# S5 output sums laid between the first steps of the triangular inverses, GLU blocks behind the products with the inverse

## The reference

```python
# gated DeltaNet: 4 heads of 128 channels, chunks of 64 tokens
lower = jnp.where(strict, einsum('bhnid,bhnjd->bhnij', k_beta, k) * decay, 0.0)
sol = triangular_solve(lower + eye, [v * beta, k_beta * exp(gc)])      # u, w
attn = einsum('bhnid,bhnjd->bhnij', q, k) * decay
# for each chunk:
v_new = u_i - w_i @ state
o = qd_i @ state + attn_i @ v_new
state = state * sd_i + kd_i.T @ v_new
# S5: 32 groups of 16 channels, each with 64 complex states
y = Re(C x) + D u ;  y = gelu(y) ;  y = y * sigmoid(y @ glu_w + glu_b)
# the two halves are concatenated and projected
return concatenate([rms_norm(o) * silu(z), y]) @ w_out
```

## Time and profile before

| what | value |
|---|---|
| median of 3 runs | 1383.79 us (1382.90 to 1386.55) |
| the profiled execution | 1378.0 us |
| its span, first to last instruction | 1376.4 us |
| PE busy | 1318.1 us, 96% |
| VectorE busy | 710.2 us, 52% |
| the changed stretch, 202 to 306 us | 104 us; PE busy 95.8, VectorE 70.8 |
| mean granted clock of PE | 0.98 |

### The profile page before, as it was taken

How to read it: one execution, slowest core, us unless ns; L and a number is a source line. 1 busy time by engine, 2 the same in 40 slices (tenths; PEclk the granted TensorE clock), 3 DMA queues, 4 the chain that set the end, 5 groups by cost and what they waited for, 6 DMA issues and landing times.

```text
span 1376.4 us, 18845 instructions
## 1 busy us (share of the span) xinstructions
PE 1318.1 (96%) x7511; PEld 1098.4 (80%) x7511; DVE 710.2 (52%) x796; ACT 504.4 (37%) x590; POOL 137.5 (10%) x225
## 2 busy tenths in 40 slices
PE   5899999899899999999999999999999999999997
PEld 3588888898778888888787888887778888888886
DVE  3789867476756633446636243345563333333353
ACT  6344642353422221222323276455432232222232
POOL 6007986000000000000000000000000000000000
PEclk9999999999899999999998999999999999999999
DMA  9484553306267642357422320211233323433122
GB/s 316 141 153 154 178 137 82 94 19 227 62 218 240 222 137 84 108 151 233 149 78 90 117 67 31 85 47 54 73 97 106 92 69 92 115 104 108 58 80 77
DMA packets 201547, 163.25 MB, mean 119 GB/s; under 512 B 25422, under 2 KB 191531, under 8 KB 199435
## 3 DMA queue, kind: packets, MB, share of 16 engines
q1 hardware_dynamic: 198256, 136.24, 34.3%
q0 software_dynamic: 2720, 25.99, 5.2%
q10 hardware_dynamic: 506, 0.12, 0.1%
HBM read 157.21 MB, written 4.19 MB: 117 GB/s over the span
## 4 chain that ended last, share of the span: by engine, by line
PE 88%; DVE 4%; ACT 2%; issue 2%; SPq 2%; DMA 1%; DVEq 0%; ACTq 0%
PE banks L487 26%; PE banks L489 25%; PE banks L488 25%; PE banks L783 2%; PE banks L1135 1%; PE banks L1108 1%; DMA ada_first<-in_ada_w_dram 1%; PE banks L493 1%; SPq L374 1%; PE banks L1126 1%; PE banks L1125 1%; SPq L348 1%; PE banks L831 1%; PE banks L773 1%; PE banks L705 0%
## 5 line engine op out<-in xcount | busy, mean ns | idle before, releaser
L487 PE MATMUL banks<-hn_hi,whi 128*128 128x512 f32 x992 | 393.4, 397 | 11.0 <-DVE hn_lo L1778 7.4
L489 PE MATMUL banks<-hn_hi,wlo 128*128 128x512 f32 x992 | 389.6, 393 | 0.0
L488 PE MATMUL banks<-hn_lo,whi 128*128 128x512 f32 x992 | 389.5, 393 | 0.0
L1756 DVE TENSOR_TENSOR wlo<-raw,whi 128x2048 fp32r<-128x2048 f32 (+3 forms) x110 | 234.0, 2129 | 124.3 <-ACT whi L1319 60.0
L1319 ACT ACTIVATE whi<-raw 128x2048 fp32r<-128x2048 f32 (+1 forms) x66 | 123.1, 1865 | 315.0 <-PE banks L489 314.8
L487 PEld LDWEIGHTS banks<-hn_hi,whi 128*128 128x128 f32 x992 | 188.7, 190 | 51.3 <-issue 11.7
L489 PEld LDWEIGHTS banks<-hn_hi,wlo 128*128 128x128 f32 x992 | 188.2, 190 | 39.8
L488 PEld LDWEIGHTS banks<-hn_lo,whi 128*128 128x128 f32 x992 | 188.9, 190 | 38.3
L487 PE MATMUL banks<-ff_hi,whi 128*128 128x512 f32 x416 | 165.7, 398 | 2.4 <-DVE ada_acc L2174 1.6
L489 PE MATMUL banks<-ff_hi,wlo 128*128 128x512 f32 x416 | 162.2, 390 | 0.0
L488 PE MATMUL banks<-ff_lo,whi 128*128 128x512 f32 x416 | 162.1, 390 | 0.0
(11 more groups left out here) (450 smaller groups left out, 1638.5 us busy)
## 6 DMA issues: line engine op xcount, KB each, us to landing
raw<-in_ffn_w_in_dram SPq DMA_DIRECT2D x88, 512.0 KB, 4.6
ada_in<-in_ada_w_dram POOLq DMA_DIRECT2D x16, 1536.0 KB, 6.3
ada_in<-in_ada_w_dram SPq DMA_DIRECT2D x24, 512.0 KB, 4.3
raw<-in_ffn_w_out_dram SPq DMA_DIRECT2D x32, 384.0 KB, 3.8
raw<-in_sb_w_in_dram SPq DMA_DIRECT2D x24, 512.0 KB, 4.1
raw<-in_hy_w_in_dram SPq DMA_DIRECT2D x20, 512.0 KB, 6.0
raw<-in_ffn_w_out_dram SPq DMA_DIRECT2D x32, 320.0 KB, 3.3
ada_first<-in_ada_w_dram SPq DMA_DIRECT2D x8, 1024.0 KB, 15.1
```

What stands on the lines that cost most here:

```text
L487: pe.matmul(o, lh, rh, start=first, stop=False)
L488: pe.matmul(o, lh, rl, start=False, stop=False)
L489: return pe.matmul(o, ll, rh, start=False, stop=last)
L1756: TTO(wlo[s][:, 0:width], raw[s][:, 0:width], whi[s][:, 0:width].bitcast(F32), SUB)\
```

## The change

1. The table `GDN_STAGES` loses `y`, and `at` moves behind `d2`, `d2t`. The S5 sums now go to banks 0 to 3.
2. The S5 sums become a function `s5_outputs(r)`, and its eight steps are laid behind `d2`/`d2t` (0, 1), `at` (2), `x1` (3, 4), `d4` (5, 6) and `x2` (7).
3. The tiles `Da`, `DaT`, `Db`, `DbT`, `X`, `XT`, `Z` move to the unused upper halves of the weight slots, so slots 12 and 13 are loaded and split later.
4. `DaT` is made by VectorE between the drains of `lt` and `l`.
5. Six tiles of the modulation and the scaling of the queries move between VectorE's drains of the inverse; the eight `mod_column` products stand together behind `z2`.
6. `u` and `w` are drained by VectorE, ahead of `ys_lo`. The GLU blocks stand behind `w` and ahead of the chunk loop.
7. On VectorE the splits of the gated S5 half (`mixed_lo`) and of slots 12 and 13 stand inside the chunk loop.

```diff
-GDN_STAGES = [("gr",), ("kt", "vt"), ("lt",), ("at",), ("y",), ("l",),
-              ("d2", "d2t"), ("x1",), ("d4", "d4t"), ("x2",), ("d8t",), ("x3",), ("xt",),
+GDN_STAGES = [("gr",), ("kt", "vt"), ("lt",), ("l",),
+              ("d2", "d2t"), ("at",), ("x1",), ("d4", "d4t"), ("x2",), ("d8t",), ("x3",), ("xt",),
...
-        Da, DaT, Db, DbT, X = (diagonal(n, o) for n, o in (("Da", 120), ("DaT", 104), ("Db", 136),
-                                                           ("DbT", 144), ("X", 128)))
+        Da, DaT, Db, DbT, X = (diagonal(n, o) for n, o in (("Da", 20), ("DaT", 28), ("Db", 36),
+                                                           ("DbT", 44), ("X", 52)))
...
             for t in range(8):
                 ada0_tile(4, t)
+            sp.wait_ge(s5_copied, 8)
             for i in range(SC):
-                if i == 0:
-                    for q in range(4):
-                        wait_drained(sp, "y", q)
...
+            sp.wait_ge(gdn_done, GDN_AT[("d8t", NH - 1)] + 1)
             for s in range(2):
                 load_slot(12 + s, s, cols(hy_w_out[0], 256 * s)(s))
...
@@ tensor @@
-                if lv == 1:
-                    pe.wait_ge(ys_done, 1)
-                    pe.wait_ge(mod_done, 3)
-                    four_blocks(10, B_GLU, ys_hi, ys_lo, k_tiles=4)
...
+            pe.wait_ge(ys_done, 1)
+            pe.wait_ge(mod_done, 3)
+            four_blocks(10, B_GLU, ys_hi, ys_lo, k_tiles=4)
 
             for c_ in range(TT):
                 for hd in range(NH):
...
-                        pe.wait_ge(block_free, B_OUT0)
+                        pe.wait_ge(block_free, B_GLU + hd + 1)
...
@@ scalar @@
-            for hd in range(NH):
-                drain_scaled("u", hd, vn, k_gain)
-                drain("w", hd, wT)
...
@@ vector @@
+            lt_drained(0)
+            lt_drained(1)
+            lower_turned(0)
+            lt_drained(2)
+            lower_turned(1)
+            lt_drained(3)
+            lower_turned(2)
+            l_drained(0)
+            lower_turned(3)
...
             onto("x2", X, ADD)
+            ada0_tile(4, 2)
             onto("x3", X, ADD)
+            ada0_tile(4, 3)
             masked(0)
+            ada0_tile(4, 4)
             onto("xc0", X, SUB)
+            ada0_tile(4, 5)
             onto("xtc0", XT, SUB)
+            masked(1)
+            ada0_tile(4, 6)
+            onto("xc1", X, SUB)
+            ada0_tile(4, 7)
...
+            lo(10, 0, 1024)
+            for hd in range(NH):
+                src, free = product("u", hd)
+                TTO(vn[:, hd, :, :], src, bc(k_gain[:, hd, :], P), MUL).then_inc(free, 1)
+                src, free = product("w", hd)
+                dve.tensor_copy(wT[:, hd, :, :], src).then_inc(free, 1)
+            lo(11, 1, 1024)
...
             for c_ in range(TT):
...
+                if c_ == 1:
+                    for r in range(4):
+                        mixed_lo(r)
+                if c_ == 2:
+                    lo(12, 0)
+                    lo(13, 1)
```

More of the change, by code:

```diff
@@ L836, in _ @@
                               start=False, stop=False)
-                for o, rows, i, g in lanes(r):
+                for o, rows, i in lanes:
                     last = pe.matmul(o[:, 0:wide * NC].rearrange("p (a c) -> p a c", c=NC)[:, :, 1:NC],
@@ L841, in _ @@
                     if r == 7:
-                        last.then_inc(gdn_done, 1)
+                        last.then_inc(s5_sum, 1)
             for hd in range(NH):
@@ L855, in _ @@
                 mul_pair("x1", hd, DbT, X)
-                if hd == 0:
-                    pe.wait_ge(block_free, B_Z + 4)
-                    pe.wait_ge(ada_used, 24)
-                for k in range(2 * hd, 2 * hd + 2):
-                    last = mod_column(3, 4, k, ada0_acc[0])
-            last.then_inc(mod_sum, 1)
+            s5_outputs(3)
+            s5_outputs(4)
             for hd in range(NH):
@@ L898, in _ @@
                     o[64:P, 0:64], LT[0:64, hd, c_, 64:P], X[0:64, hd, c_, :], start=True, stop=True))
+            pe.wait_ge(s5_copied, 8)
+            pe.wait_ge(ada_used, 24)
+            for k in range(KT):
+                last = mod_column(3, 4, k, ada0_acc[0])
+            last.then_inc(mod_sum, 1)
             for hd in range(NH):
@@ L1488, in _ @@
                 drain_pair("d8t", hd, DbT)
+            for n in range(4):
+                act.wait_ge(s5_sum, 5 + n)
+                act.activation(u_pair[:, 8 * (n // 2):8 * (n // 2) + 8, n % 2, :],
+                               bank[n].rearrange("p (g c) -> p g c", c=NC), ACT.Copy).then_inc(s5_copied, 1)
             for hd in range(NH):
                 drain_pair("xt", hd, XT)
+            hi(10, 0, 1024)
+            hi(11, 1, 1024)
+            act.preload_act_table(ACT.Gelu_apprx_tanh)
             act.wait_ge(y_in, 64)
@@ L1503, in _ @@
                 act.activation(perm(ys_hi[:, r, :]), y_s5[:, r, :, :], ACT.Copy).then_inc(glu_hi, 1)
+            act.wait_ge(gdn_done, GDN_AT[("xtc2", NH - 1)] + 1)
             hi(12, 0)
             hi(13, 1)
-            for hd in range(NH):
-                drain_scaled("u", hd, vn, k_gain)
-                drain("w", hd, wT)
             for hd in range(NH):
@@ L2009, in _, with pair, each, lt_drained @@
                 dve.tensor_copy(k_tok[:, hd, :, :], src).then_inc(free, 1)
-            for t in range(2, 4):
-                ada0_tile(4, t)
-            for hd in range(NH):
+            def pair(name, hd):
+                q, b, _ = gp(name, hd)
+                dve.wait_ge(gdn_done, q + 1)
+                return bank[b][:, 0:256].rearrange("p (c i) -> p c i", c=TT), drained[q % 4]
+            def each(m_):
+                return m_[:, 0:64].unsqueeze(1).to_broadcast([P, TT, 64])
+            def lt_drained(hd):
                 src, free = product("lt", hd)
@@ L2087, in _, with mixed_lo @@
                 TS(XTF[0:64, hd, :, 64:P], src[0:64, :, 64:P], -1.0, None, MUL).then_inc(free, 1)
-            lo(12, 0)
-            lo(13, 1)
-            for r in range(4):
+            mod_parts(2, 4, 1)
+            lo(10, 0, 1024)
+            for hd in range(NH):
+                src, free = product("u", hd)
[3 more added lines that the diff above has]
+            lo(11, 1, 1024)
+            dve.wait_ge(ys_hi_done, 1)
+            TTO(ys_lo[:, :, :], y_s5[:, :, :, :].rearrange("p k j c -> p k (j c)"),
+                ys_hi[:, :, :].bitcast(F32), SUB).then_inc(ys_done, 1)
+            dve.wait_ge(scan_done, 1)
+            dve.memset(sq_sum[:, :], 0.0).then_inc(sq_added, 8)
+            for r in range(4):
+                dve.wait_ge(block_free, B_GLU + r + 1)
+                TTO(y_s5[:, r, :, :], y_s5[:, r, :, :], tmp[r % 2][:, :].rearrange("p (j c) -> p j c", j=SC),
+                    MUL).then_inc(glu_mul, 1)
+            dve.wait_ge(glu_mul, 4)
+            def mixed_lo(r):
                 dve.wait_ge(glu_hi, r + 1)
@@ L2445, in _ @@
                 select(dec[:, hd, :, :], [[0, TT], [1, P]], 0, -1).then_inc(dec_done, 1)
-            for hd in range(NH):
-                wait_drained(pool, "lt", hd)
-                wait_drained(pool, "at", hd)
-                for n, rows in enumerate((slice(0, 64), slice(64, P))):
-                    pool.tensor_tensor(DaT[rows, hd, :, :], LT[rows, hd, :, rows],
-                                       strict_upper[rows, :].unsqueeze(1).to_broadcast([64, TT, 64]), MUL)\
-                        .then_inc(dat_done, 1)
-                    pool.wait_ge(dat_done, 2 * hd + n + 1)
             pool.wait_ge(gates, 1)
@@ L2463, in _ @@
             pool.wait_ge(rk_done, NH)
-            pool.wait_ge(gdn_done, GDN_AT[("d8t", NH - 1)] + 1)
+            pool.wait_ge(s5_sum, 8)
             pool.memset(XTF[64:P, :, :, 0:64], 0.0).then_inc(xt_zero, 1)
```

110 lines of the change are left out of this document (49 added, 61 removed).

## The result

The changed kernel takes 1401.9 us (median of 4 runs, 1397.3 to 1403.7), the kernel before on the same chip 1383.35: ratio 1.0134, 95% interval 1.0103 to 1.0166, 18.5 us slower. Forecast were 1398.5 and a range of 1389 to 1405.

A forecast was written before the change was run, and what follows sets the result against it. PE, busy 96% of the span, was taken to bound the kernel. Terms of 0.6 + 2.9 + 8.2 + 3 = 14.7 us, with the runs' offset carried over, gave 1398.5 us, 1.1% slower; 8-in-10 range 1389 to 1405 us.

The forecast's parts named there:

- Third part: Chunk loop: PE waits 3.4 and 4.2 us for drains queued behind VectorE's splits, last drains 0.6; +8.2 us.
- Second part: u, w and GLU: PE waits 4.3 us for ys_lo and 1.0 for the last sigmoid; +2.9 us in sum.
- First part: From lt to the end of the inverse: 4.3 us removed, 6.4 added, 1.5 of issue gaps saved; +0.6 us.
- rival D: Ahead of d2: S5 steps hide no wait; DaT at twice 0.43 us gives 1402 us; 11% shared with Rival B.
- The issue gaps: Long run of 64x64 products, line 783: 3.5 us of gaps now, 2 taken as left, saving 1.5 us.
- The clock: PE's lower clock after three new idle stretches (GLU, chunk loop): 0 to 7 us, 3 taken.
- Rival B: Ahead of GLU: stored S5 results return late, excess over 2 us margin counts; 1407.5 us; 11% shared with rival D.
- A: Whole stretch: waits as worked out, but clock stays up and issue gaps vanish; +8.3 us, 1392 us; 12%.
- C: Chunk loop and GLU wait: not slower, VectorE's late passes are short; +2.2 us, 1386 us; 6%.

The follow-up runs named there:

- e1: Changed kernel with VectorE's split of slot 11 and ys_lo put ahead of the u and w drains; ratio 1.0089 to the kernel before.
- e2: Changed kernel with the splits of slots 12 and 13 taken out of the chunk loop; ratio 1.0095 to the kernel before.
- e3: Changed kernel with the four mixed_lo passes behind the chunk loop and the first mixed block waiting tile by tile; ratio 1.0113 to the kernel before.
- e5: Kernel before with only the GLU blocks moved behind u and w, their later passes placed as in the change; ratio 1.0056 to the kernel before.
- e6: Changed kernel with 36 extra filler matmuls between the last w product and the wait for ys_lo; ratio 1.0151 to the kernel before.
- before_again: Kernel before, unchanged, run and profiled once more; ratio 0.999.
- e4: Changed kernel with S5 steps 0 and 1 behind lt and behind l, not behind d2; ratio 1.0109 to the kernel before.
- e8: Changed kernel with one of the eight modulation columns behind z2, seven left out; ratio 1.0108 to the kernel before.
- e9: Changed kernel in a new order of S5 steps, ada tiles, modulation columns, GLU blocks and VectorE passes; 1377.5 us, ratio 0.9972 to the kernel before.
- e7_all: Changed kernel with the edits of e1, e2, e3 and e4 together; ratio 1.0031 to the kernel before.

## Why the prediction was right

Right in sign and place: two waits in the loop, one ahead of GLU and one ahead of `d2`, and 1398.5 us against 1401.9, inside the range. In size the forecast was too low, 14.7 us against 18.5 by the medians and 19.7 to 21.1 by the profiles. The split was less good than the total: the waits were put too high and the slow clock too low, and these errors offset each other in part. By its own steps:

- **Third part, the chunk loop, +8.2 us.** Measured +8.7, but this closeness is luck: the forecast left the clock out of this term, and of the 8.7 about 2.6 us are slow clock. Both waits are where they were put, released by L2129, 2.90 and 2.84 us, 6.1 together with 0.17 each. I had 3.4 and 4.2: the second is shorter in part because the groups ahead of it ran at the low clock, 0.85 us apart, while VectorE was already on its way (3.32 in e1, where the clock stayed up). e2 and e3 took each away alone, e5 put both into the kernel before.
- **Second part, +2.9 us.** The idle time ahead of GLU is 4.12 us (forecast 4.3), the sigmoid's 0.87 (1.0 with its hand-overs). `u` to loop, less the GLU blocks with their wait in the kernel before (264.82 - 0.85 to 275.93, 11.96 us), is 27.02 - 9.67 - 11.96 = +5.4 us, and up to +7.8 with the second execution of each kernel. The difference to 2.9 is the slow clock at the first blocks (1.6 to 2.3 us by e6) and at `u` and `w`.
- **First part, +0.6 us: the term that was mis-sized.** Less the blocks' 11.96 in the kernel before, `lt` to `u` is 74.37 to 75.39 against 70.68: +3.7 to +4.7 (+2.6 to +3.6 against before_again, whose issue gaps are 1.5 us longer). The mechanism stood as forecast: the VectorE chain LT, `DaT`, `Da` makes PE wait behind `lt`, where S5 steps were at hand (e4 moved two of them there and took 4 us off). `DaT` costs 0.43 us a half, as priced, so rival D is out, though its 1402 us is the time that was measured. From `lt` to the end of `d2t` I had 12.9 us; in e8, where the clock stayed up, it is 13.05. What I left out is that the clock would fall here too: in the changed kernel it is 15.2 us, and the d2 groups ran at 0.57 of full clock, 2.9 us more than at full pace, some 2.2 net, as the slower groups wait less. e4 gave this back with the waits. Likewise the modulation columns: priced 1.6 us, they take 2.6 to 3.2 here and 1.9 at full clock (e9). Against that the waits behind the modulation tiles, ahead of `xtc0`, `z1` and `xtc1`, were priced at 1.6 us and are 0.6.
- **The issue gaps.** Taken at 2 us left of 3.5; one of 2.08 (1.80 in three of the traces). Right as a number. But the kernel before shows 3.0 and 4.5 in its two executions, so one trace was too little to price the saving from. No run shows what these gaps are.
- **The clock.** Forecast 3 us (0 to 7) for three new idle stretches. All three were followed by low windows: 1.6 to 2.3 us at GLU, about 2.6 in the loop and 0.8 to 2.2 behind it, 5 to 7 us. The Trainium skill, "TensorE: Matmul & The Clock Gate", section "HAM oscillation — how this bites in real kernels", says of a kernel with long enough waits between its bursts that PE is throttled again in each and the next burst starts cold. By that rule I would have had 18.7 us, 7 of it for the clock, and at these three waits the profile sides with it. That sum leaves out the low clock at d2 and at the columns and puts the waits too high, so it is luck that 18.7 lies so near 18.9. And there is an exception: in e1_ys_early the clock stayed at 1.00 behind the wait of 2.89 us, as it did in none of the seven other traces with this wait.

```profile
312.00:316.00 4.00, 3.75 (x32) 3.65 (x32) 3.67 (x9) 0.00 (x0) 0.00 (x0) 1.00 0.00 0
```

- **Rival B**, the late S5 half, did not come true, but by luck: y came back at 277.8, 4.3 us later than I had put it (2.4 of it the late start of `lt`), and VectorE asked at 291.2 instead of 279.4, because `u` and `w` themselves came late. In e9_new_order, where PE is early, this very wait is the one that is left. **A** and **C** fell with the low windows and with passes as long as before.

What stays open: why the clock falls behind one wait and not behind the like one in another execution. The runs show only that it varies at d2, ahead of `lt` and in the loop.

## What to carry to other kernels

Before moving a block of matmuls, list what the other engines do while it runs: the move takes the cover from them, and their passes reappear in front of whatever PE asks for next. Work that is to fill a wait must stand at the wait: two S5 steps moved 8 to 10 us earlier, to where PE waited, were worth 4 us. And measure several cures together before adding them up: each alone can count the same slow clock, and a pass that is moved out of one stretch can delay the next, as `o_n` in e7_all.
